# Window attention of 16 heads, two heads at a time: fused mask and row maximum, paired products, small sums for two heads

## The reference

```
s_loc = where(|i - j| <= 128, q k^T, -1e30)      # 256 keys of the sequence
s_ctx = q kc^T                                   # 256 keys of the context, no mask
p     = softmax(concat(s_loc, s_ctx, sink of the head))
o     = p_loc v + p_ctx vc
y     = o @ w_o
```

## Time and profile before

| | |
|---|---|
| median of 3 runs | 2604.07 us (2595.69 to 2605.29) |
| profiled execution | 2608.34 us, span 2606.4 us |
| PE busy | 2267.1 us, 87% of the span |
| DVE busy | 1048.9 us, 40% |
| ACT busy | 706.4 us, 27% |
| mean granted clock of PE | 0.946 |
| DMA | 686.92 MB, mean 264 GB/s |

### The profile page before, as it was taken

How to read it: one execution, slowest core, us unless ns; L and a number is a source line. 1 busy time by engine, 2 the same in 40 slices (tenths; PEclk the granted TensorE clock), 3 DMA queues, 4 the chain that set the end, 5 groups by cost and what they waited for, 6 DMA issues and landing times.

```text
span 2606.4 us, 35552 instructions
## 1 busy us (share of the span) xinstructions
PE 2267.1 (87%) x13940; PEld 1589.4 (61%) x13940; DVE 1048.9 (40%) x1599; ACT 706.4 (27%) x961; POOL 194.4 (7%) x339
## 2 busy tenths in 40 slices
PE   8999899989999899999959888888499779888885
PEld 7888688888888788886933333333375633333332
DVE  5556655565556555644431000000578521110001
ACT  4334443343344333432201000000345301100000
POOL 1000100000001000000001111111000011111110
PEclk9999999999999999999969999999789879999998
DMA  9775447738756277632469999999530489999996
GB/s 322 248 240 159 116 154 269 256 122 283 248 175 194 88 265 252 214 100 81 147 256 400 407 407 411 407 408 412 180 114 1 151 324 413 412 408 411 416 415 255
DMA packets 243208, 686.92 MB, mean 264 GB/s; under 512 B 29530, under 2 KB 168810, under 8 KB 188944
## 3 DMA queue, kind: packets, MB, share of 16 engines
q1 hardware_dynamic: 213584, 642.82, 65.8%
q0 software_dynamic: 13648, 20.16, 2.6%
q10 hardware_dynamic: 15856, 22.24, 2.5%
HBM read 682.70 MB, written 21.07 MB: 270 GB/s over the span
## 4 chain that ended last, share of the span: by engine, by line
PE 56%; DMA 24%; DVE 8%; issue 8%; DVEq 2%; ACT 1%; ACTq 1%; POOLq 1%; POOL 0%; SPq 0%
DMA expert_ahead<-in_w 17%; PE ps L695 13%; PE ps L696 13%; PE ps L697 13%; PE ps L1120 6%; DMA raw<-in_w 3%; PE ps L709 2%; DMA expert_rows<-work,row_of_slot_col 2%; PE ps L736 2%; PE ps L1138 1%; DVE w_lo L1831 1%; DMA router_rows<-work 1%; PE ps L1271 1%; PE ps L1286 1%; PE ps L884 1%
## 5 line engine op out<-in xcount | busy, mean ns | idle before, releaser
L1831 DVE TENSOR_TENSOR w_lo<-raw,w_hi 128x2048 fp32r<-128x2048 f32 x180 | 410.9, 2289 | 340.6 <-ACT w_hi L1328 340.1
L695 PE MATMUL ps<-t_hi,w_hi 128*128 128x256 f32 (+1 forms) x1568 | 455.1, 290 | 3.8 <-DVE w_lo L1831 3.8
L1328 ACT CAST w_hi<-raw 128x2048 fp32r<-128x2048 f32 x180 | 341.8, 1904 | 417.4 <-PE ps L697 386.4
L696 PE MATMUL ps<-t_lo,w_hi 128*128 128x256 f32 (+1 forms) x1568 | 453.4, 289 | 0.0
L697 PE MATMUL ps<-t_hi,w_lo 128*128 128x256 f32 (+1 forms) x1568 | 450.4, 287 | 0.0
L2516 DVE COPY work<-ps 128x512 f32<-128x512 f32 x64 | 44.2, 691 | 824.0 <-PE ps L1138 824.0
L695 PE MATMUL ps<-w_hi,t_hi 128*128 128x256 f32 (+1 forms) x1088 | 353.4, 325 | 20.2 <-DVE t_lo L1831 16.8
L696 PE MATMUL ps<-w_lo,t_hi 128*128 128x256 f32 (+1 forms) x1088 | 352.4, 324 | 0.0
L697 PE MATMUL ps<-w_hi,t_lo 128*128 128x256 f32 (+1 forms) x1088 | 352.4, 324 | 0.0
L1120 PE MATMUL ps<-raw,work 128*64 128x512 f32 x512 | 250.3, 639 | 73.0 <-DMA raw<-in_w 67.1
L695 PEld LDWEIGHTS ps<-t_hi,w_hi 128*128 128x128 f32 x1568 | 295.7, 189 | 23.8 <-issue 13.2
(11 more groups left out here) (336 smaller groups left out, 2409.1 us busy)
## 6 DMA issues: line engine op xcount, KB each, us to landing
expert_ahead<-in_w SPq DMA_DIRECT2D x188, 1024.0 KB, 25.8
raw<-in_w SPq DMA_DIRECT2D x128, 1024.0 KB, 25.3
work<-in_w SPq DMA_DIRECT2D x60, 1024.0 KB, 27.6
work<-in_w_mod SPq DMA_DIRECT2D x32, 1536.0 KB, 6.4
raw<-in_ffn_w_gate SPq DMA_DIRECT2D x44, 1024.0 KB, 8.8
raw<-in_ffn_w_up SPq DMA_DIRECT2D x44, 1024.0 KB, 9.8
raw<-in_ffn_w_down SPq DMA_DIRECT2D x44, 1024.0 KB, 4.9
raw<-in_w_in SPq DMA_DIRECT2D x18, 1024.0 KB, 5.3
```

Source lines behind the costliest of these rows:

```text
L695: pe.matmul(dst, a[0], b[0], start=start, stop=False)
L696: pe.matmul(dst, a[0], b[1], start=False, stop=False)
L1328: act.copy(slot(j)[0], src).then_inc(w_hi_ready, 1)
L1831: return dve.tensor_tensor(dst, src, hi.bitcast(F32), ALU.subtract)
```

## The change

Steps are now 16, one for a pair of heads and a tile of queries. Scores of a pair are two products of 64 rows in the two row halves of PE, into banks 0 and 1; there is one set of these banks, and of the banks 2 and 3 for the transposes, so scores(i + 1) wait for `s_ready` of step i and turned(i) for `aT_ready` of step i - 1. Values of a pair go to the two column halves, alternating. `mask` has 512 columns, of which DVE sets the second half to zero once; `tensor_tensor_reduce` adds it, writes the scores to SBUF and gives the row maximum, in one instruction per head. The small instructions work on two columns, in `sum_squares` (`pair_stat`); the sink's exponent is formed on DVE (one more small instruction), its exponential is one on ACT for both heads. PE's order is scores(i + 1), values(i - 2), turned(i - 1). Attended banks 0 to 2 are copied inside the loops of ACT and DVE; the last one is copied ahead of `norm_rows(11)`. The tiles `s2`, `p2` and `pT2` have moved. Of the lines that go, those not shown here are in the listing above.

```diff
@@ -274,14 +274,22 @@
...
-        window = w(R3 + 3072, 512).rearrange("p (t n) -> p t n", t=2)
+        mask = w(R3 + 3072, 1024).rearrange("p (t n) -> p t n", t=2)
...
-        s2 = w(R1, 1024).rearrange("p (b n) -> p b n", b=2)
-        p2 = w(R1 + 1024, 1024).rearrange("p (b n) -> p b n", b=2)
-        pT2 = w(R1 + 2048, 1024).rearrange("p (b n) -> p b n", b=2)
+        s2, p2, pT2 = (w(a, 2048).rearrange("p (b e n) -> p b e n", b=2, e=2) for a in (R0, R0 + 2048, R1))
+
+        def pair_stat(i, x):
+
+            return ss[:, 12 * (i % 2) + 2 * x:12 * (i % 2) + 2 * x + 2]
+
+        def sinks(i):
+
+            return rows2[:, 2 * HD + i // 2 * 2:2 * HD + i // 2 * 2 + 2]
+
+        less_sinks = rt[:, 0:HEADS2]
...
@@ -1264,38 +1272,41 @@
...
                 def scores(i):
...
+                    hp, qt = divmod(i, 2)
+                    if i >= 1:
+                        pe.wait_ge(s_ready, 16 + i)
+                    for e in range(2):
+                        mm = pe.matmul(ps[:, e, :], qT2[64 * e:64 * e + 64, hp, qt * P:(qt + 1) * P],
+                                       kT2[64 * e:64 * e + 64, hp // 2, :], start=True, stop=True)
+                    mm.then_inc(sc_ready, 1)
+
+                def turned(i):
                     pe.wait_ge(a_ready, 16 + i + 1)
+                    if i >= 1:
+                        pe.wait_ge(aT_ready, 16 + i)
+                    for e in range(2):
+                        for t in range(4):
+                            mm = pe.transpose(ps[:, 2 + e, t * P:(t + 1) * P], p2[:, i % 2, e, t * P:(t + 1) * P], ident)
+                    mm.then_inc(at_ready, 1)
+
+                def values(i):
+                    hp, qt = divmod(i, 2)
+                    pe.wait_ge(aT_ready, 16 + i + 1)
                     for t in range(4):
...
+                        for e in range(2):
+                            mm = pe.matmul(ps[64 * e:64 * e + 64, 4 + hp // 2, (hp % 2) * 256 + qt * P:(hp % 2) * 256 + (qt + 1) * P],
+                                           v2[:, t, (hp // 2) * 64:(hp // 2 + 1) * 64], pT2[:, i % 2, e, t * P:(t + 1) * P],
+                                           start=t == 0, stop=t == 3)
                     mm.then_inc(o_ready, 1)
 
                 scores(0)
-                for i in range(34):
-                    if i + 1 < 32:
+                for i in range(18):
+                    if i + 1 < 16:
                         scores(i + 1)
-                    if 1 <= i < 33:
-                        attend(i - 1)
                     if i >= 2:
                         values(i - 2)
+                    if 1 <= i < 17:
+                        turned(i - 1)
                 pe.wait_ge(ao_lo, 4 + 4)
...
@@ -1759,7 +1770,7 @@
...
-                load(w(R3 + 3072, 512), consts("window"), dftl_landed)
+                load(mask[:, :, 0:SEQ], consts("window").rearrange("p (t n) -> p t n", t=2), dftl_landed)
...
@@ -1786,26 +1797,33 @@
...
                 def exps(i):
...
+                    b = i % 2
                     act.wait_ge(s_ready, 16 + i + 1)
...
+                    act.activation(pair_stat(i, 2), pair_stat(i, 2), ACT.Exp)
+                    for e in range(2):
+                        x = act.activation(p2[:, b, e, :], s2[:, b, e, :], ACT.Exp, bias=pair_stat(i, 1)[:, e:e + 1],
+                                           accum_out=pair_stat(i, 3)[:, e:e + 1])
+                    x.then_inc(p_ready, 1)
 
                 def weights_T(i):
                     act.wait_ge(at_ready, 16 + i + 1)
...
+                    for e in range(2):
+                        x = act.copy(pT2[:, i % 2, e, :], ps[:, 2 + e, :])
+                    x.then_inc(aT_ready, 1)
+
+                def attended_hi(b):
+                    act.wait_ge(o_ready, 16 + 4 * b + 4)
+                    act.copy(t_hi[:, b * BANK:(b + 1) * BANK], ps[:, 4 + b, :]).then_inc(ao_hi, 1)
+
+                for i in range(17):
+                    if i < 16:
                         exps(i)
                     if i >= 1:
                         weights_T(i - 1)
-                act.wait_ge(o_ready, 16 + 32)
+                    if i in (7, 11, 15):
+                        attended_hi((i - 7) // 4)
+                attended_hi(3)
                 norm_rows(11)
-                for b in range(4):
-                    act.copy(t_hi[:, b * BANK:(b + 1) * BANK], ps[:, 4 + b, :]).then_inc(ao_hi, 1)
                 split(p + 9)
...
@@ -2634,41 +2652,50 @@
...
                 dve.drain().then_inc(qk2_ready, 1)
+                dve.memset(mask[:, :, SEQ:], 0.0)
                 for x in (6, 7, 8):
                     split(p + x)
                 dve.wait_ge(dftl_landed, 32)
                 dve.wait_ge(qkT_ready, 12)
 
-                def bias_and_max(i):
-                    h, qt = divmod(i, 2)
-                    b = i % 2
+                dve.tensor_scalar(less_sinks, rows2[:, 2 * HD:2 * HD + HEADS2], -1.0, None, ALU.mult)
+                dve.drain()
+
+                def mask_and_max(i):
+                    qt = i % 2
...
+                    for e in range(2):
+                        dve.tensor_tensor_reduce(s2[:, qt, e, :], ps[:, e, :], mask[:, qt, :], 1.0, -3.0e38, ALU.add, ALU.max,
+                                                 pair_stat(i, 0)[:, e:e + 1])
+                    dve.drain()
+                    dve.scalar_tensor_tensor(pair_stat(i, 1), pair_stat(i, 0), -1.0, less_sinks[:, i // 2 * 2:i // 2 * 2 + 2],
+                                             ALU.mult, ALU.min)
+                    dve.drain()
+                    dve.tensor_tensor(pair_stat(i, 2), sinks(i), pair_stat(i, 1), ALU.add).then_inc(s_ready, 1)
 
                 def weights(i):
-                    b = i % 2
                     dve.wait_ge(p_ready, 16 + i + 1)
...
+                    dve.tensor_tensor(pair_stat(i, 4), pair_stat(i, 2), pair_stat(i, 3), ALU.add)
+                    dve.drain()
+                    dve.reciprocal(pair_stat(i, 5), pair_stat(i, 4))
+                    dve.drain()
+                    for e in range(2):
+                        x = dve.tensor_scalar(p2[:, i % 2, e, :], p2[:, i % 2, e, :], pair_stat(i, 5)[:, e:e + 1], None, ALU.mult)
+                    x.then_inc(a_ready, 1)
+
+                def attended_rest(b):
                     dve.wait_ge(ao_hi, 4 + b + 1)
                     a = slice(b * BANK, (b + 1) * BANK)
                     rest(t_lo[:, a], ps[:, 4 + b, :], t_hi[:, a]).then_inc(ao_lo, 1)
+
+                for i in range(17):
+                    if i < 16:
+                        mask_and_max(i)
+                    if i >= 1:
+                        weights(i - 1)
+                    if i in (8, 12, 16):
+                        attended_rest((i - 8) // 4)
+                attended_rest(3)
                 split(p + 9)
                 gated_residual_2(p + 6)
```

More of the change, by code:

```diff
@@ L1266, in scores @@
                 def scores(i):
-                    h, qt = divmod(i, 2)
[L1268 to L1274, removed]
-                    pe.wait_ge(a_ready, 16 + i + 1)
-                    for t in range(4):
-                        mm = pe.transpose(ps[:, 2 + i % 2, t * P:(t + 1) * P], p2[:, i % 2, t * P:(t + 1) * P], ident)
+                    hp, qt = divmod(i, 2)
@@ L1788, in exps @@
                 def exps(i):
-                    h = i // 2
+                    b = i % 2
                     act.wait_ge(s_ready, 16 + i + 1)
-                    act.activation(m1[:, i % 2, 2:3], rows2[:, 2 * HD + h:2 * HD + h + 1], ACT.Exp,
-                                   bias=m1[:, i % 2, 1:2])
-                    act.activation(p2[:, i % 2, :], s2[:, i % 2, :], ACT.Exp, bias=m1[:, i % 2, 1:2],
-                                   accum_out=m1[:, i % 2, 3:4]).then_inc(p_ready, 1)
+                    act.activation(pair_stat(i, 2), pair_stat(i, 2), ACT.Exp)
[3 more added lines that the diff above has]
+                    x.then_inc(p_ready, 1)
                 def weights_T(i):
                     act.wait_ge(at_ready, 16 + i + 1)
-                    act.copy(pT2[:, i % 2, :], ps[:, 2 + i % 2, :]).then_inc(aT_ready, 1)
-                for i in range(33):
-                    if i < 32:
+                    for e in range(2):
[6 more added lines that the diff above has]
+                    if i < 16:
                         exps(i)
@@ L2654, in weights @@
                 def weights(i):
-                    b = i % 2
                     dve.wait_ge(p_ready, 16 + i + 1)
-                    dve.tensor_tensor(m1[:, b, 4:5], m1[:, b, 2:3], m1[:, b, 3:4], ALU.add)
+                    dve.tensor_tensor(pair_stat(i, 4), pair_stat(i, 2), pair_stat(i, 3), ALU.add)
                     dve.drain()
-                    dve.reciprocal(m1[:, b, 5:6], m1[:, b, 4:5])
+                    dve.reciprocal(pair_stat(i, 5), pair_stat(i, 4))
                     dve.drain()
```

(11 more changed lines are left out.)

12 lines of the change are left out of this document (removed).

## The result

| | before | after |
|---|---|---|
| median, 4 runs each, alternating | 2599.95 us (2595.69 to 2605.29) | 2566.95 us (2558.91 to 2570.05) |
| ratio, 95% interval | | 0.9864 (0.9847 to 0.9881) |
| profiled execution, span | 2608.34, 2606.4 us | 2567.25, 2565.3 us |
| first scores of attention | 1936.27 | 1935.93 |
| output projection starts | 2040.53 | 2002.77 |

Faster by 1.4%: 33 us between the medians, 35 by the ratio, 41 between the two profiled executions. Predicted were 2564 and 40. The last column of the table is read downwards: 0.3 us were there before attention, 37.4 more came in attention and its tail, 3.2 more between the projection's start and the first expert product and hardly anything after it. The expert stage, whose loads start behind the projection, simply moved (SP issues at 2025.93, 40.35 earlier than in the earlier trace rows).

What follows compares the result with a forecast made beforehand. PE and DVE, both full at 2.75 us per head, alternate as the bound; projection starting 37.6 us earlier plus 2.5 from its clock make 40.1, taking the 2604.07 median to 2564, range 2553 to 2582.

Steps and rivals of the forecast that it cites:

- PE's pieces: PE per pair of heads: scores 1.05, values 1.02, transposes 1.03, sum 3.10 us against 5.50.
- The rival of unpaired halves: PE's halves don't run side by side: 2577 us in values alone, 2587 in scores too; chance 0.07.
- DVE: DVE per pair: 3.02 us in all, scores given back 1.78 after their start.
- Half rate: Rival: DVE's fused instruction runs at half pace, 0.53 more each, loop 4.07, total 2576 us; chance 0.08.
- a slow program: Rival: DVE's fused instruction is as slow as its reciprocal, 3.4 us each, loop 8.6, total 2644; chance 0.03.
- The last wait: Attention loop: transposes wait for ACT's two copies of the previous pair, values come before them; period 3.27 us.
- Bank copies in the loop: Three attended bank copies in the loop: about 0.7 us each for two, nothing for the third; 1.4.
- Start and clock: Attention's start: first transposes at 1945.5, one pair more at low clock (2.2 us), last values end at 2001.5.
- The reason given for the shorter low clock: Attention's start: the clock returns within 6 us where whole passes follow each other; today's 21 us use half the array.
- Tail: Before the projection: PE idle 1.4 us instead of 5.4, start at 2002.9, and 2.5 us from the projection's high clock.
- The total: Whole kernel: 37.6 us up to the projection's start and 2.5 in it, together 40.1 less.

Runs made afterwards that it cites:

- the edit that takes it away alone: Kernel after, with ACT copying each head's bank as soon as PE has transposed it: 2560.89 us, period 3.10 or 3.11.
- the second series: Kernel after unchanged, measured again on one chip in 5 rounds beside the kernel before: median 2561.66 us, ratio 0.9846.
- the first series: Kernel after against the kernel before, 4 runs each, alternating: median 2566.95 us beside 2599.95, ratio 0.9864.
- fused alone: Kernel before with only mask, copy and maximum put into one DVE instruction per head: 2596.85 us beside 2595.93.
- the tail alone: Kernel before with only the four bank copies put ahead of the DMAs of norm_rows(11): 2598.84 us beside 2595.93; run again, ratio 0.9993.

## Why the prediction was right, step by step

- **PE's pieces**: scores 1.13 (predicted 1.12), transposes 1.09 (1.10), values 1.09 and 1.02 until PE goes on (1.02). Both pairings were tested by taking them away: without them 1.98 and 1.58. The rival of unpaired halves is refuted; its price was right for the scores (0.85 more for PE) and too high for the values (0.49 instead of 0.85). The Trainium skill (TensorE: Matmul & The Clock Gate, Part 3, "The mechanism") lets a weight load overlap a running matmul only where the row groups differ, and both column halves have the same ones. By that rule neither order of the values would overlap more than the other, so 1.09 against 1.58 disagrees.
- **DVE**: fused 0.69, successor after 0.61, scores given back 1.77 after their start (1.78), DVE's sum from 1976.56 to the end of its path 3.00 (3.02). Half rate (1.2) and a slow program (3.4) are refuted. The Trainium skill's rule of half throughput (Vector Engine (DVE) Microarchitecture Reference, "Points that are easy to get wrong") is of two sources in SBUF. Here one is PSUM, so 0.69 doesn't test it; only the row of 0.693 in the earlier trace rows does. And the skill says it of one instruction layout, `S2S2D2_STT`; that `tensor_tensor_reduce` has this layout, no run shows.
- **The last wait**: ACT's two copies, 3.28 (3.27). This is the term that carried the sum, and the edit that takes it away alone gives PE's sum, 3.10 (3.10).
- **Bank copies in the loop**: 0.68 each for two, nothing for the third (0.7, 0.7, 0).
- **Start and clock**: first transposes at 1945.88 (1945.5), clock back at about 1949.4 (1948), last values' end 2001.3 (2001.5). From the first to the second transposes it is 4.83, so the low clock added 1.6 to the loop and not 2.2; the start 0.4 later makes up for most of that. The reason given for the shorter low clock, products that use the whole array, isn't shown: from its fall to its return the clock was low for 13.7 us, and for 10.2, 13.7, 17.1 and 20.5 in the four traces of the old order.
- **Tail**: idle 1.41 (1.4), projection at 2002.77 (2002.9), at the high clock: its first 6.3 us at 1.00, from its first to its last product's start 22.6 us instead of 25.2, 2.6 less (2.5). In two other traces of the old order it was 24.0 and 24.1, so the clock is worth 1.4 to 2.6 there. Another 0.6 up to the first expert product wasn't forecast: 32 transposes behind the normalisation took 5.77 us instead of 6.71, with a shorter low clock. They took 5.9 to 6.7 in the traces of the old order and 5.3 to 6.3 in those of the new one, so this part scatters.
- **The total**: 41.1 less between the profiled executions (40.1). It is right for that pair and for the second series, whose ratio 0.9846 is 40 us (33 to 47); the first series' 35 us (31 to 40) is lower. That the pair agrees to 1 us is in part luck, for the clock of the kernel before was the term that was least sure: from the first scores to its return it took 21.4 us in the trace that the forecast was made against, 16.8, 11.2 and 13.5 us in the three other traces with the old order (fused alone, the tail alone twice), and 11 to 15 in those of the new order with paired scores. The two traces of the tail alone, with the 2.2 us of that edit put back, have stages of 99.7 and 101.3 instead of 104.26. Against them the change takes 32.8 and 34.4 from the stage and 2.6 and 1.4 from the projection, an estimate of 35 to 36 us in all. I took one profiled execution for typical there. Whether 35 or 40 is nearer for median executions, the two series leave open.

The mechanism of the forecast held in attention and in its tail; what was uncertain is the clock. The forecast said that relieving one of the two engines alone would gain little, and the runs put numbers on it: the fused instruction in the old order 5.32 instead of 5.50 per two heads, the new order without it 4.41 instead of 3.28.

## What to carry to other kernels

Where two engines alternate as the bound, add up each engine's own time per turn and every loop that returns through a single buffer; the new period is the largest of them. Two such sums were seen here as periods (3.27 and 3.10, measured 3.28 and 3.10) and a third in DVE's rows (3.02, measured 3.00). The sums also name the next edit before the first is run: it is the one that brings the largest down to the second largest. When the expected gain is under the scatter of single times, measure a stage between two events of the trace and not the whole, and look at the clock of that stage in several traces before one of them is taken as typical.

## What the runs showed of the hardware

- PE's granted clock: it fell to 0.50 (1.2 GHz) in an idle piece of 3.65 us or within 1.1 us behind it. From its fall to its return it was low for 10.2 us in three traces, 13.6 or 13.7 in six, 17.1 in one and 20.5 in the kernel before, and nearly the same program had different ones of these. With seven idle-filling matmuls it stayed at 1.00 (2.4 GHz). With scores in one half only it stayed at 0.50 for 31 us though PE was never idle in the last 17 of them.
- The same clock before the projection: idle pieces of 3.19 to 5.72 us were followed by 3.2 to 5.9 us of projection at 0.50 in all four traces, pieces of 1.41 or less by none in nine traces and by 3.4 in one.
- `tensor_tensor_reduce` with add and max, one source in PSUM and one in SBUF, 128x512 float32: 0.69 us, 0.61 from start to start, 0.08 for the accumulator read behind it. A maximum over 1024 columns: 1.22.
- Two column halves with 64 rows of output each: 16 records in 1.09 us alternating, 1.58 in turn. Two row halves: four records of 512 columns in 1.13 us side by side, 1.98 in one half.
- One and the same program on one chip: 2594 to 2612 us over 17 runs.
